# Paged sample attention: issuing the page gathers at another point of the loop, and copying the turned probabilities in three pieces

## The reference

```python
past_c = cache_kv_latent[l, page_table].reshape(DB, past_len, KV_LORA)      # 2048 x 256 for each sample
past_kpe = cache_k_rope[l, page_table].reshape(DB, past_len, ROPE_DIM)      # 2048 x 64
s_past = (einsum('bqhc,bkc->bhqk', q_lat, past_c) + einsum('bqhr,bkr->bhqk', q_pe, past_kpe)) * MLA_SCALE
...
pr = softmax(concatenate([s_past, s_new], axis=-1), axis=-1)
return einsum('bhqk,bkc->bqhc', pr[..., :P], past_c) + einsum('bhqk,bkc->bqhc', pr[..., P:], c_kv)
```

## Time and profile before

| | |
|---|---|
| median of 3 runs | 1956.11 us (1955.09 to 1959.73) |
| the profiled execution | 1960.08 us, its span 1958.3 us |
| TensorE matmul busy | 1812.6 us, 93% of the span |
| VectorE, ScalarE, GpSimd busy | 688.0, 481.7, 112.3 us |
| mean granted TensorE clock | 0.974 of full speed |
| sample attention | about 553 to 660 us of the span |

### The profile page before, as it was taken

One profiled execution on the slowest core, in us unless ns is written; L12 is line 12 of the kernel. 1 busy time (PEld: TensorE's weight loads), 2 busy tenths in 40 slices (PEclk: granted clock), 3 DMA queues, 4 the chain that ended last, 5 costly groups with the idle time before them and its releaser, 6 DMA issues.

```text
span 1958.3 us, 35913 instructions
## 1 busy us (share of the span) xinstructions
PE 1812.6 (93%) x15607; PEld 1242.8 (63%) x15607; DVE 688.0 (35%) x1296; ACT 481.7 (25%) x836; POOL 112.3 (6%) x115
## 2 busy tenths in 40 slices
PE   6999997997989999898999999999999999999994
PEld 5999997875666799686455554444554444554541
DVE  4437776545566543754411111111111111111113
ACT  4446653341222422732311111011000000000001
POOL 0000002300101000000000000000000000000000
PEclk7999999898999999999999999999999999999998
DMA  7644540214535673548899999999999999999995
GB/s 220 158 131 123 145 122 4 67 30 130 162 117 209 190 218 84 172 120 320 310 374 429 421 423 427 423 396 406 421 423 426 421 420 397 413 422 427 422 425 201
DMA packets 191392, 545.99 MB, mean 279 GB/s; under 512 B 39227, under 2 KB 146844, under 8 KB 163566
## 3 DMA queue, kind: packets, MB, share of 16 engines
q1 hardware_dynamic: 184080, 518.03, 69.3%
q0 software_dynamic: 6768, 26.09, 4.3%
q10 hardware_dynamic: 438, 0.32, 0.1%
HBM read 524.86 MB, written 28.06 MB: 282 GB/s over the span
## 4 chain that ended last, share of the span: by engine, by line
DMA 28%; PE 21%; DVE 1%; issue 1%; SPq 0%; DVEq 0%
DMA w_expert<-in_w_up_dram 27%; PE p_u L2951 8%; PE p_y L2967 4%; PE p_g L2951 4%; PE p_xg L2919 3%; DMA w_expert<-in_w_down_dram 1%; PE p_xgT L2934 1%; PE p_g L2926 0%; DVE w_expert L3112 0%; DVE w_expert L3121 0%; PE p_xgT L2940 0%; PE p_xgT L3026 0%; PE p_y L2974 0%; PE p_xg L3026 0%; DVE y_slots L3067 0%
## 5 line engine op out<-in xcount | busy, mean ns | idle before, releaser
L2951 PE MATMUL p_u<-w_expert,xgT 128*64 128x256 f32 x2048 | 239.6, 388 | 34.0 <-DMA w_expert<-in_w_up_dram 33.9
L2951 PE MATMUL p_g<-w_expert,xgT 128*64 128x256 f32 x2048 | 232.0, 379 | 0.9 <-DVE xgT L3051 0.9
L2951 PEld LDWEIGHTS p_u<-w_expert,xgT 128*64 128x64 f32 x2048 | 148.4, 140 | 117.8 <-DMA w_expert<-in_w_up_dram 43.5
L2967 PE MATMUL p_y<-w_expert,hidT 128*64 128x512 f32 x960 | 217.8, 595 | 0.8 <-DVE hidT L3063 0.5
L2951 PEld LDWEIGHTS p_g<-w_expert,xgT 128*64 128x64 f32 x2048 | 147.1, 137 | 87.5 <-issue 18.4
L2919 PE MATMUL p_xg<-low,slot_sel 128*64 128x512 f32 x768 | 177.9, 598 | 0.0
L2967 PEld LDWEIGHTS p_y<-w_expert,hidT 128*64 128x64 f32 x960 | 66.2, 137 | 126.0 <-issue 124.1
L3056 DVE CAST row<-rowf 128x1 int32<-128x1 f32 x32 | 4.9, 153 | 355.9 <-POOLq L3193 355.9
L3141 ACT ACTIVATE act_g<-p_g 128x256 f32<-128x256 f32 x32 | 12.3, 384 | 449.5 <-PE p_u L2951 449.5
L2919 PEld LDWEIGHTS p_xg<-low,slot_sel 128*64 128x64 f32 x768 | 52.5, 137 | 80.7 <-issue 74.2
L426 PE MATMUL in_acc<-x_high,w_in_high 128*128 128x320 f32 (+2 forms) x560 | 93.9, 320 | 8.2 <-ACT w_in_high L458 8.2
(11 more groups left out here) (601 smaller groups left out, 2480.9 us busy)
## 6 DMA issues: line engine op xcount, KB each, us to landing
w_expert<-in_w_gate_dram SPq DMA_DIRECT2D x64, 2048.0 KB, 21.7
w_expert<-in_w_up_dram SPq DMA_DIRECT2D x64, 2048.0 KB, 23.3
w_expert<-in_w_down_dram SPq DMA_DIRECT2D x60, 2048.0 KB, 20.5
w_in_raw<-in_w_in_dram SPq DMA_DIRECT2D x32, 1024.0 KB, 5.8
ho_raw<-in_w_out_dram SPq DMA_DIRECT2D x12, 1024.0 KB, 6.5
q_lat<-in_w_out_dram SPq DMA_DIRECT2D x4, 1024.0 KB, 8.3
mem_k_s<-in_cache_mem_k_dram SPq DMA_DIRECT2D x8, 512.0 KB, 7.0
mem_v_s<-in_cache_mem_v_dram SPq DMA_DIRECT2D x8, 512.0 KB, 11.9
```

The source lines that it names most:

```text
L2951: mm = pe.matmul(acc[SL * h:SL * h + SL, 0:FF // 2], xgT[:, t, g // 2, :], w[g][:, FF * t + FF // 2 * h:FF * t + FF // 2 * h + FF // 2], s ...
L2967: mm = pe.matmul(p_y[SL * h:SL * h + SL, 512 * b:512 * b + 512], hidT[:, j, g, :], tile, start=(g == 0 and j == 0), stop=(g == 1 and j == 1))
```

## The change

The gathers of samples 3 to 7 wait for one more semaphore, `new_copied`, so that gather b is issued once the own probabilities of sample b-2 have been turned and copied, which is in iteration b-1 just ahead of the value products. And `p_pt` is copied in three pieces of 256, 256 and 512 columns instead of two of 512, each raising `p_copied`, so the counts that TensorE waits for go by three per sample.

```diff
@@ mla_sample, gpsimd
                     else:
                         pool.wait_ge(made, b - NBUF + 1)
+                        pool.wait_ge(new_copied, b - NBUF + 2)
                     gather_pages(pool, d, S, b, last_row)
@@ turn_probabilities
                     if b:
-                        pe.wait_ge(p_copied, 2 * b)
+                        pe.wait_ge(p_copied, 3 * b)
@@ values
                     for j in range(8):
-                        if j % 4 == 0:
-                            pe.wait_ge(p_copied, 2 * b + j // 4 + 1)
+                        if j in (0, 2, 4):
+                            pe.wait_ge(p_copied, 3 * b + j // 2 + 1)
@@ copies
                     act.copy(p_newT[:, :], p_o[0:64, 384:448]).then_inc(new_copied, 1)
-                    for u in range(2):
-                        act.wait_ge(p_turned, 3 * b + 2 + u)
-                        act.copy(probT[:, 4 * u:4 * u + 4, :].rearrange("p j n -> p (j n)"), p_pt[:, 512 * u:512 * u + 512]).then_inc(p_copied, 1)
+                    act.wait_ge(p_turned, 3 * b + 2)
+                    for j, n in ((0, 2), (2, 2), (4, 4)):
+                        if j == 4:
+                            act.wait_ge(p_turned, 3 * b + 3)
+                        act.copy(probT[:, j:j + n, :].rearrange("p j n -> p (j n)"), p_pt[:, 128 * j:128 * j + 128 * n]).then_inc(p_copied, 1)
```

## The result

| | before | changed |
|---|---|---|
| median of 4 runs | 1957.92 us (1955.09 to 1961.38) | 1982.03 us (1976.53 to 1982.75) |
| profiled execution, its span | 1960.08, 1958.3 us | 1982.75, 1981.0 us |
| sample attention, from the issue of gather 2 to SyncE's first load for the next block | 102.16 us | 125.91 us |

The ratio is 1.0119, with a 95% interval of 1.0102 to 1.0136: slower by some 24 us. In the profile after it runs from 555.31 to 681.22; before it ran from 558.64 to 660.80. The blocks before this stage vary by some us from one execution to the next, and so do the experts behind it, so that one span is a poorer measure of a change in this stage than the stage itself.

What follows compares the result with a forecast made beforehand. TensorE, busy 93% of the span, was taken to bound the kernel, and the gather's place to have no slack. Loops +28.5, scores of sample 2 -1.8, pieces -0.4 gave +26.3 us: 1982.4 us, range 1974 to 1990.

Steps and rivals of the forecast that it cites:

- Five closed loops: Gathers 3 to 7, copy to copy: five loops of 9.47 us plus landing, 92.15 us against 63.65, loss 28.5 us.
- Reaction: GpSimd starts the gather 0.29 us after the copy that releases it ends, in each loop.
- Landing: Latent gather from issue to landing: 8.96 us in the mean, 44.8 us for five.
- Scores behind the wait: TensorE's score products after idling for keys, with the step to the own keys: 6.69 us per loop.
- The rival with the clock staying down: TensorE holds 1.2 GHz through all scores to the next copy: +39 us in all, 1995 us; chance 0.06.
- First key block and the end of the loop: Loop terms: first key block turned and loaded 0.73 us; own keys to copied own probabilities 1.71 us.
- Scores of sample 2: Scores ahead of the first moved gather are rid of gather 3: -1.80 us.
- the price: A gather at the start of the score products costs TensorE 1.80 us, five times over.
- Pieces: A 128x256 copy takes 0.37 us, values start 0.22 us earlier; counts for samples 0 and 6 only, -0.4 us.
- After the stage: No late stage can use anything in flight, so the sample attention's loss is passed on whole.
- The faster rival: Landing short enough under the value products, break-even 4.2 us: saves 10.5 us, 1945.6 us; chance 0.03.
- The idle wait: Added wait already met when value products end, so only the pieces act: 1.5 us, 1954.6 us; chance 0.03.

Runs made afterwards that it cites:

- one_wait: Changed kernel with the gathers' wait for the value products removed, leaving the wait for new_copied alone: 1981.26 us, ratio 1.0159, stage 125.73 us.
- mid8: Changed kernel, but gather b waits until eight of the ten key blocks of sample b-1 are used, in place of both waits: 1965.52 us, stage 109.44 us.
- wait_only: Kernel before with only the gathers' additional wait for new_copied, copies still in two pieces: 1979.74 us, ratio 1.0149, stage 127.03 us.
- pieces_only: Changed kernel without the additional wait for new_copied, so three-piece copies alone, on chip 2: 1948.37 us, ratio 0.999, stage 93.45 us.
- pieces_again: Same kernel as pieces_only, run again on chip 4: 1958.37 us, ratio 0.9993 to before, stage 101.16 us.
- warm: Changed kernel with 19 additional unused 128x64 by 128x256 products behind the values of samples 1 to 5: 1991.02 us, stage 133.49 us.

## Why the prediction was right

The forecast, +26.3 us and 1982.4, met +24.1 and 1982.03, by the mechanism that it named. That the two totals are 0.4 us apart is luck: the loss was forecast 2.2 us too high and the median of before came out 1.8 us higher than the one that it was added to, and within the loss three errors partly cancel (reaction +2.4, landing -3.7, scores -1.6). Term by term, with the loops from the profile after:

- **Five closed loops.** Forecast 92.15 us, measured 667.98 - 578.59 = 89.39, where before 63.65. So 25.7 us instead of 28.5.
- **Reaction.** 0.29 forecast, 0.77 measured, +2.4 in five loops. The row of before was of a single wait; one_wait shows that the second wait in GpSimd's queue is the cause.
- **Landing.** 44.8 forecast from the old place, 8.7 + 8.2 + 8.5 + 7.8 + 7.9 = 41.1 measured, -3.7. The landing of gather 7, 10.3 before, is 7.9 now. A gather of one place differs from another by as much (7.8 to 9.8 us in one_wait), so that an effect of the place is not shown. The Trainium skill, "DMA: Bandwidth & Descriptors", section "Anatomy of one DMA — SWDGE (gpsimd) path", gave an estimate of 6.8; even with the rotary gather left out the traces have 7.9 to 8.8 in the new place and 9.0 to 9.5 in the old, so it is too low here.
- **Scores behind the wait.** 5 x 6.69 = 33.5 forecast, 5.96 + 7.40 + 6.34 + 6.16 + 6.02 = 31.9 measured. In the 5.96 one VectorE set the pace: last key turned at 594.37, own keys 0.68 behind; and 5.96 is what the same work took at full clock in mid8, four times. So the excess over 5.96, 2.1 us in sum, is what half clock costs in this kernel. The clock is a term, and not the loss. The rival with the clock staying down, 0.06, is refuted: of the 7.40 us stretch, the worst, the mean granted clock is 0.60 and not 0.50, and the end of the loop kept its 1.71 us.
- **First key block and the end of the loop.** 0.73 and 1.71 forecast; 0.76 (588.33 to 589.09) and 1.71 (595.05 to 596.76).
- **Scores of sample 2.** -1.80 forecast and found on chip 1, 4.51 against 6.30. But I took for a property of the kernel what comes and goes with the chip: on chip 2 this term is 0, and wait_only and one_wait lost 29 and 30 us there, some 5 to 6 us more than the changed kernel on chip 1. The prediction was given for a trace that had the price, and was timed where before had it; on chip 2 its sum would have been too low. The cover that I counted on, 5 us of room for the gather's disturbance of the value products, was not needed: these products took 3.60 us with the gather as without.
- **Pieces.** 0.37 us interpolated, 0.376 measured. I was wrong that the trace of before has no such copy: L1190 copies 128x256 out of TensorE's result in 0.372 to 0.375 us. Copy to values is 1.10 us (578.59 to 579.69) against 1.32, the 0.22 that I had.
- **After the stage.** Passed on: +23.75 in the stage, +22.7 in the span, +24.1 in the medians.
- **The faster rival** needed a landing under 4.2 us; of gathers 3 to 7 in all the runs none is under 7.7. **The idle wait** is refuted by the row of gather 3 in GpSimd's timeline, which waits for p_newT.

## What to carry to other kernels

Before a transfer is moved to a quieter place, measure its lead: from its issue to the first use of its data. Here it was 9.3 us for a landing of 8 to 10. The change let gather 3 leave some 8.4 us later in its iteration, and the loops paid 5.1 us each for it, once per iteration, since the late transfer closes a loop of its own with the work that releases it. And a stall that comes in every iteration of one profile need not belong to the kernel; run the unchanged kernel on another chip before building on it.

## What was not expected of the hardware

- TensorE loses 1.8 to 1.9 us per score stretch of 160 products when two gathers are issued within it in the runs called chips 1, 3 and 4, and nothing on chip 2, with the same code in pieces_only and pieces_again: 4.50 against 6.4 us. One gather alone costs 0.75. The value products lose nothing under the same gathers (3.60 us with and without).
- A second wait ahead of a gather, though it was met 6 us or more before the one that releases the gather, costs GpSimd 0.5 us between that releaser and the start of the gather (0.77 against 0.26).
- Taking away the second gather, 0.52 of 2.62 MB and issued 1.3 us behind the first, does not bring the first 2.10 MB sooner (five landings 41.4 us without it, 40.2 in warm and 41.1 in the changed kernel with it).
- TensorE was at half clock behind each wait of 4.45 to 5.36 us in the changed kernel, and at full clock behind those of 1.1 to 1.4 us in mid8. The time to return varies within one execution: scores of 5.96 to 7.40 us.
